# Sixteen modulation sums of the first mixer: VectorE multiply-and-add against GpSimd product and ScalarE sum

## The reference, cut to what matters

```
mod = einsum('bd,ldm->lbm', silu(c), w_mod) + b_mod      # per layer: 6 sections of 1024
for i in range(DEPTH):
    sh_m, sc_m, g_m, sh_f, sc_f, g_f = split(mod[i], 6)
    h = x * (1 + sc_m) + sh_m
    y = even_mixer(h) if i % 2 == 0 else odd_mixer(h)
    x = layer_norm(ALPHA * x + (1 + g_m) * y, ...)
    h = x * (1 + sc_f) + sh_f
    y = swiglu(h, ...)
    x = layer_norm(ALPHA * x + (1 + g_f) * y, ...)
```

## Time and profile before

| | |
|---|---|
| median of 3 runs | 1200.36 us (1199.11 to 1201.03) |
| the profiled execution's own time | 1200.52 us |
| its span, first to last instruction | 1198.7 us |
| granted TensorE clock, mean | 0.991 |
| busy: PE, PEld | 1149.8 us (96%), 1088.2 us (91%) |
| busy: DVE | 878.9 us (73%) |
| busy: ACT | 616.6 us (51%) |
| busy: POOL | 70.6 us (6%) |

### The profile page before, as it was taken

How to read it: one execution, slowest core, us unless ns; L and a number is a source line. 1 busy time by engine, 2 the same in 40 slices (tenths; PEclk the granted TensorE clock), 3 DMA queues, 4 the chain that set the end, 5 groups by cost and what they waited for, 6 DMA issues and landing times.

```text
span 1198.7 us, 22749 instructions
## 1 busy us (share of the span) xinstructions
PE 1149.8 (96%) x8630; PEld 1088.2 (91%) x8630; DVE 878.9 (73%) x1486; ACT 616.6 (51%) x989; POOL 70.6 (6%) x134
## 2 busy tenths in 40 slices
PE   4999989999999999899999999999999999999997
PEld 4898679999888898799998889999999999999997
DVE  5799788998887985696554577787764766777643
ACT  4547546444336566654443465544443646555532
POOL 0101110211111310000000000000000000000000
PEclk9899989999999999999999999999999999999999
DMA  9947656999874743476455334433333453555531
GB/s 365 413 167 264 237 202 221 367 394 356 291 300 141 248 157 120 155 281 219 175 179 206 141 121 148 156 139 107 141 141 106 164 187 111 207 180 192 188 141 36
DMA packets 43131, 241.67 MB, mean 202 GB/s; under 512 B 5152, under 2 KB 7584, under 8 KB 20400
## 3 DMA queue, kind: packets, MB, share of 16 engines
q1 hardware_dynamic: 28912, 191.29, 44.3%
q0 software_dynamic: 14144, 49.37, 11.6%
HBM read 237.48 MB, written 1.06 MB: 199 GB/s over the span
## 4 chain that ended last, share of the span: by engine, by line
PE 82%; DVE 8%; ACT 5%; issue 3%; DMA 1%; SPq 0%; POOL 0%; DVEq 0%; ACTq 0%; POOLq 0%
PE acc L1914 20%; PE acc L1915 19%; PE acc L1916 19%; PE aux L2024 3%; PE aux L2026 3%; PE aux L2025 3%; PE aux L2401 2%; DVE wlo L1043 2%; ACT whi L583 1%; DMA x<-xT 1%; PE aux L1916 1%; PE aux L1914 1%; PE aux L1915 1%; ACT free_hlo L628 1%; PE aux L2055 1%
## 5 line engine op out<-in xcount | busy, mean ns | idle before, releaser
L1914 PE MATMUL acc<-hhi,whi 128*128 128x256 f32 (+3 forms) x1976 | 567.2, 287 | 6.8 <-DVE hlo L1064 4.0
L1915 PE MATMUL acc<-hlo,whi 128*128 128x256 f32 (+3 forms) x1976 | 560.2, 283 | 0.0
L1916 PE MATMUL acc<-hhi,wlo 128*128 128x256 f32 (+3 forms) x1976 | 557.7, 282 | 0.0
L1043 DVE TENSOR_TENSOR wlo<-raw,whi 128x1024 fp32r<-128x1024 f32 x338 | 412.8, 1223 | 178.6 <-ACT whi L583 178.1
L583 ACT ACTIVATE whi<-raw 128x1024 fp32r<-128x1024 f32 x338 | 357.1, 1057 | 189.7 <-PE acc L1916 119.4
L1914 PEld LDWEIGHTS acc<-hhi,whi 128*128 128x128 f32 x1976 | 374.0, 189 | 12.0 <-DVE hlo L1064 6.2
L1916 PEld LDWEIGHTS acc<-hhi,wlo 128*128 128x128 f32 x1976 | 375.7, 190 | 0.0
L1915 PEld LDWEIGHTS acc<-hlo,whi 128*128 128x128 f32 x1976 | 374.5, 190 | 0.2
L1072 DVE CUSTOM_DVE_ANT_0 lev<-lev,vec 128x1024 f32<-128x1024 f32 x56 | 71.7, 1280 | 1.9 <-DMA lev<-side_weights 1.9
L2026 PE MATMUL aux<-wlo,ahi 128*128 128x512 f32 x176 | 69.5, 395 | 0.0
L2024 PE MATMUL aux<-whi,ahi 128*128 128x512 f32 x176 | 69.4, 394 | 0.0
(11 more groups left out here) (372 smaller groups left out, 1518.0 us busy)
## 6 DMA issues: line engine op xcount, KB each, us to landing
raw<-weights SPq DMA_DIRECT2D x171, 1024.0 KB, 4.8
lev<-side_weights POOLq DMA_DIRECT2D x76, 512.0 KB, 6.0
qkv<-weights SPq DMA_DIRECT2D x3, 1024.0 KB, 14.6
x<-ln_rows POOLq DMA_DIRECT2D x6, 512.0 KB, 6.6
lev<-weights SPq DMA_DIRECT2D x2, 1024.0 KB, 20.1
big<-side_weights POOLq DMA_DIRECT2D x4, 512.0 KB, 5.7
big<-qkv POOLq DMA_DIRECT2D x32, 64.0 KB, 2.5
x<-gate_rows POOLq DMA_DIRECT2D x3, 512.0 KB, 6.9
```

The costliest lines, as they stand in the source:

```text
L1043: v.tensor_tensor(wlo[:, m % SPLIT, :], raw_unit(i, m), whi[:, m % SPLIT, :].bitcast(F32), ALU.subtract).then_inc(lo_ready, 1)
L1914: mm(o, whi[:, u % SPLIT, w], hi, start=start, stop=False, skip_group_check=True)
L1915: mm(o, whi[:, u % SPLIT, w], lo, start=False, stop=False, skip_group_check=True)
L1916: return mm(o, wlo[:, u % SPLIT, w], hi, start=False, stop=stop_, skip_group_check=True)
```

## The change

Sixteen of the 24 sides of the first mixer (0 to 7, and the odd ones from 9 to 23) are no longer summed by VectorE. GpSimd multiplies the weights with the row silu(c) in place in the ring (`multiply`), and ScalarE adds the products up with a Copy that has an accumulator output, in the slots of `POOL_SUM_AT`: 6 to 13, 16, 18 to 24. The bias of these columns is added by VectorE in two small instructions (`add_bias`, slots 14 and 25). VectorE keeps sides 8, 10, ... 22, one each in slots 15 and 17 to 23. GpSimd's loads now alternate with its products, and a load that reuses a buffer waits for the sum of ScalarE or of VectorE, whichever used it.

```diff
-SIDE_AT = [5, 5, 15, 16, 17, 17, 18, 18] + [u for u in range(19, 27) for _ in range(2)]
+BY_POOL = list(range(8)) + list(range(9, 24, 2))
+BY_VECTOR = [n for n in range(80) if n not in BY_POOL]
+POOL_SUM_AT = [6, 7, 8, 9, 10, 11, 12, 13, 16, 18, 19, 20, 21, 22, 23, 24]
+SIDE_AT = [15, 17, 18, 19, 20, 21, 22, 23]
...
             def even_then(u):                                  # ScalarE
 
+                for at_ in at_slot(POOL_SUM_AT, u):
+                    n = BY_POOL[at_]
+                    part = mod_ring[SIDE_SLOT[n]]
+                    act.wait_ge(side_multiplied, at_ + 1)
+                    A(part, part, ACT.Copy, accum_out=mods[:, 2 * KT + n:2 * KT + n + 1]).then_inc(side_summed, 1)
...
             def sections_made(n):                              # VectorE
 
-                dve.wait_ge(side_used, KT * (n - 2))
+                last = KT * (n - 2)
+                taken = len([m for m in BY_VECTOR if m < last])
+                if taken:
+                    dve.wait_ge(side_used, taken)
+                dve.wait_ge(side_summed, len([m for m in BY_POOL if m < last]))
+
+            def add_bias(a, b, step, count):
+
+                dve.wait_ge(side_summed, count)
+                columns_ = mods[:, 2 * KT + a:2 * KT + b:step]
+                st(v.tensor_tensor(columns_, columns_, V("b_mod", 2 * KT, b)[:, a:b:step], ALU.add))
+                st.wait()
...
                 for n, at_ in enumerate(SIDE_AT):
                     if at_ == u:
-                        side_sum(n)
-                        if n == KT - 1:
-                            make_gate(0, 2)
+                        side_sum(BY_VECTOR[n])
+                if u == POOL_SUM_AT[KT - 1] + 1:
+                    add_bias(0, KT, 1, KT)
+                    make_gate(0, 2)
+                if u == POOL_SUM_AT[-1] + 1:
+                    add_bias(KT + 1, 3 * KT, 2, len(BY_POOL))
...
                     if side_last(n) is not None:               # GpSimd, load_sides
-                        pool.wait_ge(side_used, side_last(n) + 1)
+                        m = side_last(n)
+                        pool.wait_ge(side_summed if m in BY_POOL else side_used, side_taken(m))
...
+            def multiply(n):
+
+                pool.wait_ge(side_loaded[SIDE_SLOT[n]], 16 * side_turn(n))
+                part = mod_ring[SIDE_SLOT[n]]
+                nc.gpsimd.tensor_tensor(part, part, silu_rows[0], ALU.mult).then_inc(side_multiplied, 1)
+
             load_sides(0, 5)
             load_gain(0)
-            load_sides(5, 13)
-            write_gate(0)
-            load_sides(13, 15)
-            read_gate(0)
-            load_sides(15, 28)
+            for n in range(24):
+                if n in BY_POOL:
+                    multiply(n)
+                if n:
+                    load_sides(n + 4, n + 5)
+                if n == 10:
+                    write_gate(0)
+                if n == 13:
+                    read_gate(0)
             load_shift(0)
```

More of the change, by code:

```diff
@@ L129, in side_turn, with side_taken @@
     return SIDE_SLOT[:n + 1].count(SIDE_SLOT[n])
+def side_taken(n):
+    return len([m for m in (BY_POOL if n in BY_POOL else BY_VECTOR) if m <= n])
 def side_last(n):
@@ L332, in build @@
         names = """hi_ready lo_ready units_done small_loaded cst_loaded masks_loaded levels_loaded x_loaded meta_loaded row_loaded pos_loaded act_step dve_step pool_step
-            csilu_ready row_moved last_loaded first_loaded2 first_loaded3 first_loaded4 first_loaded5 first_loaded6 first_loaded7 first_used first_mm side_loaded0 side_loaded1 side_loaded2 side_loaded3 side_loaded4 side_used mods_ready affine_ready rows_loaded gate_ready gate_written gate_loaded gain_loaded shift_loaded rows_used nm_ready rs_ready u_first u_ready tr_mm
+            csilu_ready row_moved last_loaded first_loaded2 first_loaded3 first_loaded4 first_loaded5 first_loaded6 first_loaded7 first_used first_mm side_loaded0 side_loaded1 side_loaded2 side_loaded3 side_loaded4 side_used side_multiplied side_summed mods_ready affine_ready rows_loaded gate_ready gate_written gate_loaded gain_loaded shift_loaded rows_used nm_ready rs_ready u_first u_ready tr_mm
             x_norm h_f32 hhi_ready h_ready angles_ready trig_ready
@@ L344, in build @@
         (hi_ready, lo_ready, units_done, small_loaded, cst_loaded, masks_loaded, levels_loaded, x_loaded, meta_loaded, row_loaded, pos_loaded, act_step, dve_step, pool_step,
-         csilu_ready, row_moved, last_loaded, first_loaded2, first_loaded3, first_loaded4, first_loaded5, first_loaded6, first_loaded7, first_used, first_mm, side_loaded0, side_loaded1, side_loaded2, side_loaded3, side_loaded4, side_used, mods_ready, affine_ready, rows_loaded, gate_ready, gate_written, gate_loaded, gain_loaded, shift_loaded, rows_used, nm_ready, rs_ready, u_first, u_ready, tr_mm,
+         csilu_ready, row_moved, last_loaded, first_loaded2, first_loaded3, first_loaded4, first_loaded5, first_loaded6, first_loaded7, first_used, first_mm, side_loaded0, side_loaded1, side_loaded2, side_loaded3, side_loaded4, side_used, side_multiplied, side_summed, mods_ready, affine_ready, rows_loaded, gate_ready, gate_written, gate_loaded, gain_loaded, shift_loaded, rows_used, nm_ready, rs_ready, u_first, u_ready, tr_mm,
          x_norm, h_f32, hhi_ready, h_ready, angles_ready, trig_ready,
```

## The result

The changed kernel takes **1223.21 us** (median of 3 runs, 1222.07 to 1224.96) against 1200.36: ratio 1.0194, 95% interval 1.017 to 1.0217. The profiled run took 1224.96 us, with a span of 1223.2. The forecast was 1210.6 and the range ended at 1219.0. The sign was right, the loss more than twice as large, 22.9 us in place of 10.2.

A forecast was written before the change was run, and what follows sets the result against it. TensorE bounds the kernel; VectorE's sums hold it up ahead of normalize(0). Early 8.0, late 3.5 and ScalarE 0.5, less 1.8 at the end, give +10.2 on 1200.4: 1210.6 us, range 1197.5 to 1219.

The forecast's parts named there:

- The meeting: A GpSimd product running beside VectorE's work on two SBUF tensors, 60.7 to 86.2 us: 1.5 us delay each.
- A: Rival: GpSimd and VectorE don't hinder each other; 1199.1 us, or 1197.5 if the clock stays up; chance 0.22.
- B: Rival: meetings of GpSimd products with VectorE cost 0.4 us each; 1202 to 1205 us; chance 0.12.
- C: Rival: GpSimd too slow, ScalarE waits in slots 7 to 13; 1213 to 1220 us; chance 0.18, with whole-product meetings.
- absorbed in gaps: VectorE idle taking in early delay: 1.0 us at 59.60, 0.56 at 90.11 and about 0.1 more.
- product 9: GpSimd's product falling in slots 14 to 18, where ScalarE leads: cost 0.
- products 21, 23: Two late GpSimd products, coming behind VectorE's own sum: 0.2 us each.
- overlap: 1.1 of 4.6 us of late product delay, taken to fall together with the late ScalarE of slot 18.
- Early: First eight products delay VectorE's rotary work, splits and masks, from 50 us on: +8.0 us, all on the path.
- two-thirds discount: Between 60.7 and 86.2 us, two thirds of a 2.25 us product counted as VectorE delay: 1.5 us.
- Late: Products from weight 9 on delay VectorE's sum, splits and L1418 in the loop: +3.5 us.
- End: Last product 0.15 us earlier and normalize(0) starting early, as in the second mixer, 1.67 us: 1.8 us gained.

The follow-up runs named there:

- e1: The changed kernel with GpSimd's sixteen products replaced by one-column memsets, all else kept: 1200.24 us, ratio 1.0012.
- e10: The changed kernel with GpSimd's products kept only for weights 0 to 7, one-column memsets for the later eight: 1214.57 us, ratio 1.0144.
- e9: The changed kernel plus dummy matmuls in TensorE's waits, 8 ahead of slot 15 and 4 ahead of suffix sums of heads 3 to 5: 1221.15 us, ratio 1.0185.
- e11: The changed kernel with GpSimd's products kept only for weights 9 to 23, one-column memsets for the first eight: 1211.93 us, ratio 1.0113.
- e8: The kernel before, with VectorE's last sums moved out of slots 25 and 26, up to three a slot: 1198.93 us, ratio 0.9999.
- e4: The changed kernel with each GpSimd product cut into four instructions of 256 elements: 1226.4 us, ratio 1.0232.
- e2: The changed kernel with each GpSimd product replaced by three memsets of the same buffer: 1200.22 us, ratio 1.0014.

## Why the prediction was wrong

**What held.** VectorE is hindered by GpSimd's reads in two-tensor operations, and not in MAX8. One-tensor TENSOR_SCALAR operations, which the prediction didn't consider, are hindered as well (4.6 of the 25.2 us below). A product was put at 2.25 us and takes 2.4 to 2.5. The 4.5 us that the prediction takes from the Trainium skill (GPSIMD Engine Reference, section 3.1) are given there for an addition of 2048 elements, not for a product; half of it, as an estimate, is 0.1 us under the shortest product here. The meeting was put at 1.5; over all sixteen products the excess of VectorE's longer operations in after is 25.2 us, 1.58 each. L1056 and L1353 rows of 2 to 3.4 us, TensorE waiting between 65 and 90 us and 6.9 us to the first transpose came as told. The mask came later (99.89 us for 93 to 97) and turns were longer (10.4 and 10.0 us for 7 to 8). A and B fell by these rows and by e1, and C by ScalarE's 1.9 us of waiting, none of it in slots 7 to 13. Meetings that cost the whole product, which the prediction counted into C's chance, are what came for products 2 to 4.

**What failed was mainly the step from VectorE's excess to the path:** delay counted as absorbed that wasn't, and the lower clock behind new waits, put at nothing. A smaller part is the price of a meeting itself, too low for products 2 to 4. The terms, by the lags in the table and the splits between its rows (over e1 unless said):

| term | forecast | measured |
|---|---|---|
| products 0, 1 net of two sums | +0.6 | +0.9 |
| products 2, 3, 4 | 3 x 1.5 = 4.5 | 8.0 |
| products 5, 6, 7 | 3 x 1.5 = 4.5 | 2.1 + 0 + 1.1 |
| absorbed in gaps | -1.6 | 0 |
| low clock and gaps early (e10) | none | +3.9 |
| product 9 (e9) | 0 | +1.5 |
| products 11, 13 (e9) | 0 | 0 |
| product 15 (e9) | 1.2 | 1.3 |
| products 17, 19 (e9) | 1.5 each | 1.8 and 2.1 |
| products 21, 23 (e9) | 0.4 | 1.4 |
| overlap | -1.1 | 0 |
| low clock late (after over e9, 13th to 19th split) | none | +3.5 |
| ScalarE, net of the sums gone (e1 over before, 23rd split) | +0.5 | +0.3 |
| end (e1 over before, median) | -1.8 | not found |

*Early, 8.0 in the forecast, 16.0 in e10's profile.* The two-thirds discount for one-tensor work was an average over 60.7 to 86.2 us. But three of the six products fell before the search began, into a run of L1353 and L1356 with no MAX8 between them, and cost 2.67 us each, the whole product and a little more. The timeline of before has that order; the sum went by the groups of the earlier trace rows, which don't. Then the absorbed part. The idle 1.00 us at 59.60 lies ahead of products 2 to 4 and couldn't take in any of their delay. The prediction looked at the splits' lead of three units and called VectorE "full, yet not late". The result that TensorE wanted first was another, the rotary output, with 0.85 us of slack. Third, a wait of 7.07 us was never priced: the matmuls behind it ran at 0.50. How much of the 3.9 us in the table is the clock and how much are gaps that open elsewhere isn't told apart; 2.8 of it comes behind the mask wait, and in e9, with the clock held there, the 13th split isn't late by it (14.6 against 16.8). Without these 3.9 us the early products cost 12.1 us, about the half more that the prediction named for meetings that cost a whole product.

*Late, 3.5 in the forecast, 10.3 in e11's profile.* By e9, where the clock is held, products cost 21.3 - 13.3 = 8.0 us: the forecast was right on the loop (products 15, 17, 19) and wrong to put product 9 at 0, because VectorE had no lead left at slot 14 (TensorE wanted the mask 0.7 us after it was made, as the prediction itself says), to put products 21 and 23 at 0.4 for 1.4, and to let 1.1 us fall together. The other 5.7 us of after's 27.0 are the clock: 2.2 behind the wait for the mask (e10 shows them as part of its 3.9) and 3.5 in the turns up to the 19th split, behind waits for L1442. No term stood for it.

*End, -1.8.* The pattern of the second mixer showed up in the profiles of after, e1 and e8 (6.9 us to the first transpose), and not in time: e8 at 0.9999, e1 at 1.0012. A stretch at the lower clock comes behind the same 2.0 us in some profiles and not in others, e1's own executions differ in mean clock (0.988 to 0.994), and reading 1.67 us out of one profile was too much trust in it. That e1 isn't faster also shows the ceiling: taking 16 sums off VectorE was worth nothing in the median even with products that cost nothing.

Open: why the medians have 23.0 us over e1 where the profiles have 28.1. e1's profile is 3.2 us under its own median, and after's 1.8 us over; that makes up the 5 us, and what sets the clock in a given execution wasn't found. The profiles of e10 and e11 are also the shortest executions of their four, 2.1 and 3.5 us under the medians. So the table's late and clock terms hold for these profiles. For the medians the runs show +14.3 us for the early half where +8.0 was counted and +11.7 for the late half where +3.5 was, and 1 to 2 us, not told apart from none, for the clock that e9 held up.

## What to carry over

Before work is given to GpSimd, look which of VectorE's operations read two SBUF tensors, or are a TENSOR_SCALAR, in the slots where it would run, one by one in the timeline: each product costs VectorE its whole length if there is no work of another kind, such as the MAX8 search, between them. The slack to compare it with is that of the first result that the bound engine takes from VectorE after that point, not the lead of the largest stream. And price a new wait of TensorE twice, once for its length and once for the matmuls behind it that may run at the lower clock.

## What of the hardware was not expected

- Splitting GpSimd's work doesn't reliably let a waiting VectorE in: in e4 one VectorE operation took 3.54 us beside four back-to-back quarters of 2.82 us, while two splits at 53.17 us alternated with quarters, and the sum of the excess stayed (25.7 against 25.2 us). When VectorE holds the pair first, it is GpSimd's product that stretches, to 2.80 us beside 85.52.
- On GpSimd an operation with one input took longer (2.79 us) than the product of two tensors of the same size (2.4 us), and hindered VectorE less (at most 1.6 us a row; 10.0 us in all against 25.2).
- VectorE operations with one tensor are not all free: L1452, a TENSOR_SCALAR over 256 elements (0.35 us in the earlier trace rows), took 2.96 us beside a product and 1.52 us beside memsets, which read nothing, while MAX8 kept its 0.61.

```profile
128.05 2.96 DVE L1452 TENSOR_SCALAR std<-std,small 128x256 f32<-128x256 f32 x1
```

- The length of a wait didn't set the length of the stretch at the lower clock behind it: behind TensorE's wait of 1.96 to 1.99 us in normalize(0) it was about 7, about 3.5 or 0 us in seven profiles (e8 and e2; e1 and e9; after, e10 and e11).
